# Splitting weights one unit earlier, transposing the identity while waiting, and choosing experts with a match-and-replace

## The reference

```
h = x
a = rms_norm(h, norm1);  h = h + hybrid_mixer(a)          # GLA branch + dilated window attention, gated, one output product
c = rms_norm(h, norm2);  h = h + memory_cross_attention(c, mem)   # 4 heads of 128, 256 memory tokens
f = rms_norm(h, norm3);  h = h + moe_ffn(f)               # top 4 of 32 experts, gates = softmax over the 4 logits
out = rms_norm(h, final)
```

## Time and profile before

| | |
|---|---|
| median of 3 runs | 1260.05 us (1258.52 to 1261.59) |
| the profiled execution | 1258.43 us, span of its instructions 1256.7 us |
| TensorE clock granted, mean | 0.981 |
| PE (matmul) busy | 1146.3 us, 91% |
| DVE (VectorE) busy | 412.7 us, 33% |
| ACT (ScalarE) busy | 259.6 us, 21% |
| read from HBM | 456.57 MB |

### The profile page before, as it was taken

One profiled execution on the slowest core, in us unless ns is written; L12 is line 12 of the kernel. 1 busy time (PEld: TensorE's weight loads), 2 busy tenths in 40 slices (PEclk: granted clock), 3 DMA queues, 4 the chain that ended last, 5 costly groups with the idle time before them and its releaser, 6 DMA issues.

```text
span 1256.7 us, 16017 instructions
## 1 busy us (share of the span) xinstructions
PE 1146.3 (91%) x6642; PEld 569.8 (45%) x6642; DVE 412.7 (33%) x809; ACT 259.6 (21%) x449; POOL 18.5 (1%) x41
## 2 busy tenths in 40 slices
PE   6999999998999999999889988798898999889987
PEld 5788989887433333333233322332332233223332
DVE  6689464665413221121122211211211122122113
ACT  5556464355310010010001000100110010001001
POOL 3000000000000000000000000000000000000000
PEclk9999999999999999999999999999999999999999
DMA  8464524984599999999999999999999999999995
GB/s 294 185 212 177 189 78 155 387 329 159 196 378 415 434 428 431 431 434 431 433 432 431 431 430 433 430 431 431 427 431 433 433 434 433 433 432 426 430 420 233
DMA packets 27525, 458.38 MB, mean 365 GB/s; under 512 B 3296, under 2 KB 3312, under 8 KB 7504
## 3 DMA queue, kind: packets, MB, share of 16 engines
q1 hardware_dynamic: 26496, 455.09, 86.5%
q0 software_dynamic: 832, 2.51, 0.6%
q10 hardware_dynamic: 144, 0.02, 0.0%
HBM read 456.57 MB, written 1.05 MB: 364 GB/s over the span
## 4 chain that ended last, share of the span: by engine, by line
PE 62%; DMA 25%; DVE 4%; ACT 3%; issue 2%; DVEq 0%; POOL 0%; SPq 0%; POOLq 0%; ACTq 0%
DMA ring<-in_w_gate_up 25%; PE bank L1814 24%; PE bank L1836 12%; PE bank L1413 6%; PE bank L1492 5%; PE bank L1436 5%; PE bank L1775 3%; PE bank L1765 2%; DVE ring L903 1%; PE bank L1827 1%; ACT ring L591 1%; PE bank L1552 1%; PE bank L1788 1%; PE bank L1577 0%; ACT reg_a L849 0%
## 5 line engine op out<-in xcount | busy, mean ns | idle before, releaser
L1814 PE MATMUL bank<-ring,reg_a 128*64 128x512 f32 x2032 | 461.5, 605 | 49.2 <-DMA ring<-in_w_gate_up 48.4
L1814 PEld LDWEIGHTS bank<-ring,reg_a 128*64 128x64 f32 x2032 | 145.6, 139 | 346.8 <-issue 273.0
L1836 PE MATMUL bank<-ring,reg_g 128*64 128x512 f32 x1024 | 235.2, 613 | 18.5 <-DVE reg_g L1332 17.6
L1306 DVE COPY reg_t<-bank 128x512 f32<-128x512 f32 x32 | 22.1, 692 | 600.2 <-PE bank L1814 600.2
L1836 PEld LDWEIGHTS bank<-ring,reg_g 128*64 128x64 f32 x1024 | 73.7, 141 | 158.9 <-issue 140.6
L903 DVE SCALAR_TENSOR_TENSOR ring<-ring 128x2048 f16<-128x2048 f32 x47 | 107.4, 2290 | 52.6 <-ACT ring L591 52.3
L573 ACT ACTIVATE reg_t<-bank 128x512 f32<-128x512 f32 x64 | 38.2, 597 | 415.2 <-PE bank L1814 217.8
L591 ACT ACTIVATE ring<-ring 128x2048 f16<-128x2048 f32 x47 | 89.3, 1906 | 28.5 <-PE bank L1492 20.8
L863 ACT ACTIVATE reg_g<-reg_g 128x256 f32<-128x256 f32 x64 | 26.7, 416 | 303.2 <-DVE reg_g L1323 303.1
L1775 PE MATMUL bank<-reg_t,reg_g 64*128 64x512 f32 x256 | 63.6, 615 | 5.6 <-ACT reg_t L573 5.6
L1413 PE MATMUL bank<-reg_a,ring 128*128 128x256 f16 x576 | 65.4, 275 | 0.1
(11 more groups left out here) (255 smaller groups left out, 710.0 us busy)
## 6 DMA issues: line engine op xcount, KB each, us to landing
ring<-in_w_gate_up SPq DMA_DIRECT2D x54, 4096.0 KB, 29.5
ring<-in_w_down SPq DMA_DIRECT2D x27, 4096.0 KB, 29.9
ring<-in_w_dense SPq DMA_DIRECT2D x47, 1024.0 KB, 4.9
ring<-in_w_gate_up SPq DMA_DIRECT2D x14, 2048.0 KB, 11.8
ring<-in_w_down SPq DMA_DIRECT2D x7, 2048.0 KB, 14.8
ring<-in_w_gate_up SPq DMA_DIRECT2D x12, 512.0 KB, 18.7
ring<-in_w_down SPq DMA_DIRECT2D x8, 512.0 KB, 12.5
ring<-in_w_gate_up SPq DMA_DIRECT2D x4, 1024.0 KB, 27.1
```

The source lines that it names most:

```text
L1814: ins = mm(pt[nh][col:col + 64, :], xg[:, c, j * SLOTS:(j + 1) * SLOTS], loaded(v + i, C, c), start=(c == 0), stop=(c == C - 1))
L1836: ins = mm(pt[2][64 * nh:64 * nh + 64, :], actT[:, 4 * i + c, :], w[:, nh * 512:(nh + 1) * 512], start=(i == 0 and c == 0), stop=(i == 1 a ...
```

## The change

- The units `xv1` and `xq0` change places in `HALVES`; `xt0` moves ahead of `xs2` in `FILLS` and in TensorE's program.
- TensorE transposes the identity 26 times into the last bank before the transposes of x.
- VectorE scales both tiles of x.
- VectorE's splits of units 1 to 3 come ahead of the rotary arguments, unit 4 behind them; ScalarE splits up to unit 4 ahead of the sines.
- In cross-attention ScalarE and VectorE split `xo0` one place earlier (ahead of `x_values(1)` and `x_max(0)`); `xo1` is split by ScalarE ahead of `x_queries(1)` and by VectorE between the two `out_low`. ScalarE copies head 0's transposes ahead of `x_exp(2)`.
- The mask comes from replacing the four largest logits (`match_replace`) and comparing with the logits; gates are the exponentials of all 32 logits times the mask, divided by their sum.
- Slots count from 1, so `place` isn't lowered by 1. The f16 parts of h are written in four pieces on ScalarE, the first low piece is taken ahead of the logits.

```
+WARM = 26
-HALVES += [f"mix{q}" for q in range(4)] + ["xv0", "xv1", "xq0", "xq1", "xo0", "xo1"]
+HALVES += [f"mix{q}" for q in range(4)] + ["xv0", "xq0", "xv1", "xq1", "xo0", "xo1"]
-FILLS += ["xv10", "xq0", "xv11", "xs0", "xs1", "xq1", "xs2", "xs3", "xt0", "xt1", "xpv0", "xt2", "xt3", "xpv1"]
+FILLS += ["xv10", "xq0", "xv11", "xs0", "xs1", "xq1", "xt0", "xs2", "xs3", "xt1", "xpv0", "xt2", "xt3", "xpv1"]
...
 # (ScalarE)
             act.activation(cut[0][:, 0, 0:AHEAD], raw[0][:, 0:AHEAD], ACT.Copy, scale=WS).then_inc(ahead_act, 1)
-            act.wait_ge(root_done, 1)
-            act.activation(xn[:, 1, :], h[:, 1, :], ACT.Copy, scale=st[:, 1:2]).then_inc(ahead_act, 1)
...
-            cut_ahead("q_g")
-
+            cut_ahead("v_g0")
             for i in range(2):
                 act.wait_ge(trig_in, i + 1)
                 act.activation(cs[:, i, :], trig[:, 2, :], ACT.Sin).then_inc(trig_out, 1)
...
-            cut_ahead("xv1")
+            cut_ahead("xq1", 0)
...
             x_values(0)
             x_queries(0)
+            cut_ahead("xo0", 0)
             x_values(1)
...
             x_exp(0)
             x_exp(1)
-            cut_ahead("xq1")
+            cut_ahead("xo1", 0)
             x_queries(1)
+            x_probs_T(0)
             x_exp(2)
-            x_probs_T(0)
+            x_probs_T(1)
             x_exp(3)
-            x_probs_T(1)
...
-            for t in range(TT):
-                act.activation(f16[:, 0, t], h[:, t, :].rearrange("p (c n) -> p c n", c=C), ACT.Copy,
-                               scale=st[:, 6 + t:7 + t]).then_inc(f_high, 1)
+            for part in range(2):
+                cc = slice(4 * part, 4 * part + 4)
+                for t in range(TT):
+                    act.activation(f16[:, 0, t, cc], h[:, t, :].rearrange("p (c n) -> p c n", c=C)[:, cc], ACT.Copy,
+                                   scale=st[:, 6 + t:7 + t]).then_inc(f_high, 1)
...
-                act.activation(g4[:, t, :], top[:, t, 0:TOPK], ACT.Exp, bias=st[:, 52 + t:53 + t],
-                               accum_out=st[:, 54 + t:55 + t]).then_inc(top_exp, 1)
+                act.activation(e_gate[:, t, :], logit[:, t, :], ACT.Exp, bias=st[:, 52 + t:53 + t])\
+                    .then_inc(top_exp, 1)
...
 # (VectorE)
-            dve.tensor_scalar(xn[:, 0, :], h[:, 0, :], st[:, 0:1], None, ALU.mult).then_inc(norm_xn, 1)
+            for t in range(TT):
+                dve.tensor_scalar(xn[:, t, :], h[:, t, :], st[:, t:t + 1], None, ALU.mult).then_inc(norm_xn, 1)
...
-            cut_ahead("q_g")
+            cut_ahead("k_g")
...
-            cut_ahead("k_g")
-
-            dve.wait_ge(consts, 8)
+            cut_ahead("v_g0")
+
+            dve.wait_ge(consts, 7)
...
-            cut_ahead("xv1")
+            cut_ahead("xo0", 0)
...
             x_prob(0)
             x_prob(1)
-            cut_ahead("xq1")
...
             out_low("xpv0", oxT, 0)
+            cut_ahead("xo1", 0)
             out_low("xpv1", oxT, 1)
             for n in range(2):
-                cut_ahead(f"xo{n}")
...
             routed_T(3)
+            dve.memset(ranked[:, :, 0:TOPK], -FAR)
...
             dve.wait_ge(root_done, roots[0])
+            f_low_part(0, 0)
             b = take(dve, "rl")
...
             for t in range(TT):
                 ins = dve.max(top[:, t, :], logit[:, t, :])
             link(ins)
+            dve.tensor_scalar(st[:, 52:54], top[:, :, 0], -1.0, None, ALU.mult).then_inc(top_ready, 1)
+            link(dve.memset(top[:, :, TOPK:], -FAR))
             for t in range(TT):
-                ins = dve.max_index(idx_u[:, t, :], top[:, t, :], logit[:, t, :])
+                ins = dve.match_replace(left[:, t, :], top[:, t, :], ranked[:, t, :], FAR)
             link(ins)
-            link(dve.tensor_copy(idx_f, idx_u[:, :, 0:TOPK]))
-            dve.tensor_scalar(st[:, 52:54], top[:, :, 0], -1.0, None, ALU.mult).then_inc(top_ready, 1)
-            hot, hot_g = oneh[:, 0:TT * TOPK, :], oneh[:, TT * TOPK:, :]
-            link(dve.tensor_tensor(hot, mid(iota_e[:], TT * TOPK), bc(idx_f.rearrange("p a b -> p (a b)"), E),
-                                   ALU.is_equal))
-            dve.reduce_sum(mask, hot.rearrange("p (t k) e -> p t e k", t=TT), AX).then_inc(gate_ready, 1)
-            f_lows(0)
+            dve.tensor_tensor(mask, logit, left[:, :, TOPK:], ALU.not_equal).then_inc(gate_ready, 1)
+            f_low_part(0, 1)
...
-            link(dve.tensor_scalar(place, place, -1.0, None, ALU.add))
...
+                link(dve.tensor_tensor(gate, e_gate, mask, ALU.mult))
+                link(dve.reduce_sum(st[:, 54:56], gate, AX))
                 link(dve.reciprocal(st[:, 54:56], st[:, 54:56]))
-                link(dve.tensor_tensor(g4, g4, bc(st[:, 54:56], TOPK), ALU.mult))
-                link(dve.tensor_tensor(hot_g, hot, bc(g4.rearrange("p a b -> p (a b)"), E), ALU.mult))
-                dve.reduce_sum(gate, hot_g.rearrange("p (t k) e -> p t e k", t=TT), AX).then_inc(gate_ready, 1)
+                dve.tensor_tensor(gate, gate, bc(st[:, 54:56], E), ALU.mult).then_inc(gate_ready, 1)
...
 # (TensorE)
             pe.wait_ge(consts, 1)
+            for _ in range(WARM):
+                pe.transpose(pt[BANKS - 1][:, 0:P], ident[:], ident[:])
...
             feature_major("xq1", weights("xq1"), aT, C)
+            x_transposes(0)
             x_scores(2)
             x_scores(3)
-            x_transposes(0)
             x_transposes(1)
```

More of the change, by code:

```diff
@@ L65 @@
 NEG = -1.0e30
+FAR = 3.0e38
 GLA_SCALE = DK ** -0.5
@@ L1217, in routed_T, with f_low_part @@
                                   bc(g3[:, 2 * q:2 * q + 2], T), ALU.mult).then_inc(free_bank(f"f_T{q}"), 1)
-            def f_lows(part):
+            def f_low_part(part, t):
                 cc = slice(4 * part, 4 * part + 4)
-                for t in range(TT):
-                    dve.wait_ge(f_high, t + 1)
-                    hh = h[:, t, :].rearrange("p (c n) -> p c n", c=C)
-                    dve.scalar_tensor_tensor(f16[:, 1, t, cc], hh[:, cc], st[:, 6 + t:7 + t], f16[:, 0, t, cc],
-                                             ALU.mult, ALU.subtract).then_inc(f_low, 1)
+                dve.wait_ge(f_high, TT * part + t + 1)
+                hh = h[:, t, :].rearrange("p (c n) -> p c n", c=C)
+                dve.scalar_tensor_tensor(f16[:, 1, t, cc], hh[:, cc], st[:, 6 + t:7 + t], f16[:, 0, t, cc],
+                                         ALU.mult, ALU.subtract).then_inc(f_low, 1)
             routed_T(1)
@@ L1264, in gates_and_lows @@
             def gates_and_lows():
-                f_lows(1)
+                for t in range(TT):
+                    f_low_part(1, t)
                 dve.wait_ge(top_exp, 2)
+                link(dve.tensor_tensor(gate, e_gate, mask, ALU.mult))
+                link(dve.reduce_sum(st[:, 54:56], gate, AX))
                 link(dve.reciprocal(st[:, 54:56], st[:, 54:56]))
-                link(dve.tensor_tensor(g4, g4, bc(st[:, 54:56], TOPK), ALU.mult))
-                link(dve.tensor_tensor(hot_g, hot, bc(g4.rearrange("p a b -> p (a b)"), E), ALU.mult))
-                dve.reduce_sum(gate, hot_g.rearrange("p (t k) e -> p t e k", t=TT), AX).then_inc(gate_ready, 1)
+                dve.tensor_tensor(gate, gate, bc(st[:, 54:56], E), ALU.mult).then_inc(gate_ready, 1)
             def body(n, k, z, first, last):
@@ L1463, in _ @@
             feature_major("k_g", weights("k_g"), aT, C)
-            pe.wait_ge(consts, 8)
+            pe.wait_ge(consts, 7)
             pe.wait_ge(alr_cut, 2)
@@ L1629, in _ @@
             token_major("xv0", weights("xv0"), memT, C, (0, 1), 256)
-            norm_transposes("c_T", lambda t, c: xn[:, t, c * P:(c + 1) * P], ((norm_xn, 4), (norm_xn, 5)))
+            norm_transposes("c_T", lambda t, c: xn[:, t, c * P:(c + 1) * P], ((norm_xn, 5), (norm_xn, 6)))
             w_xv1 = weights("xv1")
```

24 lines of the change are left out of this document (10 added, 14 removed).

## The result

| | before | after |
|---|---|---|
| median, on one chip | 1259.72 us (4 runs, 1258.52 to 1261.59) | 1252.14 us (4 runs, 1251.61 to 1253.44) |
| profiled execution, span | 1258.43, 1256.7 | 1252.26, 1250.5 |
| granted clock, mean | 0.981 | 0.975 |

The ratio is 0.9946, with an interval of 0.9934 to 0.9958: 5.3 to 8.3 us faster. A second measurement of the changed kernel on another chip gave 0.9945 (0.9932 to 0.9958). The forecast was 1254.5, 5.5 us less than the 1260.05 before it, in a range of 1251.5 to 1258.0.

What follows compares the result with a forecast made beforehand. The prediction took a TensorE-bound front, which releases a DMA-bound stream of expert weights, to bound the kernel. First projections -2.9, cross-attention -1.8 and routing -0.8 summed to -5.5, from 1260.05 to 1254.5 us, range 1251.5 to 1258.0.

Steps and rivals of the forecast that it cites:

- What bounds it: Whole kernel: a TensorE-bound front up to the first expert's matmuls sets when the DMA-bound weight stream at 432 GB/s starts.
- A, -2.9: First projections: reordered weight splits remove TensorE's waits at v_g1 and r_g0; -2.9 us, bounds -2.0 and -2.93.
- the tightest slack is 0.9 to 1.9 us: First projections: unit 5's low half ready at 40.0 to 41.0, needed by r_g1 at 41.89, so no new wait.
- Term: 0, whatever it gains: Start up to k_g at 20.05: normalised tiles and identity transposes gain nothing, since k_g waits for unit 1; 0 us.
- B, -1.8: Cross-attention: reordered splits and copies bring xo's late pairs sooner; -1.8 us, bounds -2.2 and -0.9.
- +0.7: Cross-attention: loss at xv10, which must wait for unit 44's low half after xq0 and xv1 change places; 0.7 us.
- C, -0.8: Routing: replacement instead of index search and one-hot makes the mask earlier; -0.8 us, bounds 0 and -1.0.
- The sum: Whole kernel: -2.9 - 1.8 - 0.8 = -5.5 us, median from 1260.05 to 1254.5.
- the likeliest case: Whole run: the forecast itself, 1254.5 us, own range 1252.6 to 1257.5 with the spread of runs; chance 0.65.
- No block failed: Rival: r_g1 waits again or x_max(0) falls on the path; 1257.4 or 1256.3 us, chance 0.2.
- The stream hid nothing: Rival: the front's gain is hidden because the expert weight stream does not start earlier; 1260 us, chance 0.07.
- The clock did not stay low: Rival: TensorE's clock stays at its lower level from q_g on, price +8 us; 1262.5 us, chance 0.03.

Runs made afterwards that it cites:

- gt_first: Changed kernel with VectorE's split of unit eg3 behind the low parts of the gated output and first two transposed-probability copies in dilated attention; 1252.41 us, ratio 0.9946.
- no_warm_slack: Changed kernel without the 26 identity transposes, unit 4 split behind the sines (ScalarE) and behind the masks (VectorE); 1251.72 us, ratio 0.9945.
- b_undone: Changed kernel with cross-attention's old order of xv1, xq0, xt0, the xo0 and xo1 splits and ScalarE's copies; 1256.13 us, ratio 0.9973.
- delay_5: Kernel of no_warm_slack with 46 more identity transposes ahead of xv0, to delay the front; 1256.74 us, ratio 0.9971.
- pad_nops: Kernel of no_warm_slack with 52 empty TensorE instructions in the place of the 26 transposes; 1254.71 us, ratio 0.9958.
- alr_late: Changed kernel with ScalarE's splits of units 1 and 2 and VectorE's of unit 1 ahead of the small weights; 1253.32 us, ratio 0.9948.
- all_three: Kernel of best with the 26 identity transposes put back; 1250.40 us, ratio 0.9934.
- best: Changed kernel without identity transposes, units 3 and 4 split behind sines and masks, q_g's high parts before small weights, gates' copy before a split; 1251.22 us, 0.9942.

## Why the prediction was right, and where it was not

- **What bounds it.** The two parts, a front that sets the start and a stream that follows at its own length, are borne out by all rows of the table: 922.5 within 1.6 by the medians, 917.6 to 920.0 in the profiled executions. The stream kept its 432 GB/s.
- **A, -2.9.** Measured -3.01 and -2.86 in the two profiles of the changed kernel and 2.96 when undone. Both waits went, none came in their place in these two (0.17 did in gt_first), and the gain passed on to 150 us.
- **A, the slack.** The step "the tightest slack is 0.9 to 1.9 us" was mis-sized: it was 0.46. I let ScalarE begin unit 4 at 25.35, when it had a free place; the load was the later, at 26.70. The table load and the sines, queued behind that split, were late by as much, and the masks came at 36.3, the late end of the 35.3 to 36.3 that I had said. From there unit 5 took 5.1 us where I had put 4.7. That the term held all the same rests on a margin of half a microsecond: it was not far from failing.
- **A, "Term: 0, whatever it gains".** `k_g` stayed at 19.98, as said. The claim holds where unit 5 has slack and `k_g` waits for the small load (no_warm_slack, 49.41). In the order of the changed kernel the one profile without the transposes was 1.05 later, not 0, since unit 4's load came later and the slack was used up; with `k_g`'s wait gone they gave 0.3. x_T's 14 transposes did get shorter in the changed kernel's first profile, 2.27 for 3.25 us, but that is not steady: of the eight profiles with the 26, five have 1.75 to 2.72 for the 14, and three have 3.78 to 3.91 for all 16, where those without have 3.50 to 3.82. The Trainium skill ("TensorE: Matmul & The Clock Gate", Part 4) has it that transposes don't count as work for the clock gate. This case speaks against it: at 0.23 each the 26 would take 6.0 us, they took 4.49 to 5.81 in the eight profiles, and TensorE had done nothing else. The shortest but one, in b_undone, with x_T behind it at the full rate:

```profile
1.59 4.52 PE L1448 MATMUL bank<-ident 128*128 128x128 f32 x26 [1.59 <-POOL ident L517]
...
9.80 1.75 PE L1443 MATMUL bank<-ident,reg_g 128*128 128x128 f32 x14 [0.23 <-DVE reg_g L945]
```
- **B, -1.8.** Measured -1.96 from `c_T` to the late pairs, with +0.61 at `xv10` in it (foretold +0.7). `x_max(0)` stood behind a split, and TensorE did not wait for it.
- **C, -0.8.** Measured -0.94 to the prefix sums, and nothing more behind them (4.68 us to the first expert product in both kernels), as said: the pieces of the f16 parts and the slots from 1 gave TensorE nothing. The replacement is 0.09 + 0.18 a pair, the 0.27 taken. The Trainium skill ("Vector Engine (DVE) Microarchitecture Reference", 3.9) tells of one steady pass, and the trace is in keeping with it: 0.18 for 36 elements, as for the search over 32.
- **The sum.** -5.5 foretold, -5.7 to -5.9 at the first expert at equal clock (330.66 and 330.82 for 336.55). The medians moved by 7.1 to 7.6, so that 1252.14 lies near the low end of the range (1251.5) and below the 1252.6 that I gave as the low end of the likeliest case. The 1.2 to 1.9 between front and medians is within the interval. In the two profiled executions of the result there is almost nothing between: they differ by 6.2, of which 5.9 is the front at equal clock and 0.3 lies behind it (918.5 and 918.2), while the fall of the clock cost each of them 1.6 to 1.7. How often the clock falls differs from execution to execution and is part of what makes single medians uncertain. Whether there is more than the front in the medians stays open.
- **The rivals.** No block failed. The stream hid nothing (delay_5, by the spans; its medians don't tell). The clock did not stay low.

## What to carry to other kernels

When a wait is removed by moving a step forward, look at what now stands behind that step on its engine, and whether the step itself waits for a load: the loads' landing, not the engine's free time, sets the slack. Where a long stream follows a front, compare kernels by the start of the stream at equal clock; it told differences of 1 us where medians of five runs on different chips can be 3 us apart with the same front (no_warm_slack and pad_nops). A stand of 7 us in the middle of a stream that is bound by DMA can cost nothing, while 1 us ahead of it costs 1 us.

## What the hardware showed that was not expected

- The granted clock fell from 2.4 to 1.2 GHz at places that change between executions of one program (173 us in one, 352 in another), each in the front or at the first `down` products, after a wait of TensorE of 1.8 to 2.4 us, at 1.2 to 1.7 us a time. Two of the 14 profiles show no such fall with the same waits, three show two. With the wait at 0.67 to 0.68 (three profiles) it did not fall at the second dilated scores; with 2.12 to 2.14 it fell there in five of eleven.
- Transposes brought the rate of TensorE up: 26 of them, with nothing before, took 4.49 to 5.81 us in eight profiles, for 6.0 at the 0.23 each of a start without them.
- TensorE stood 5.3 to 5.7 us at the exit of the first loop in the kernels without the transposes at the start, and 10.8 to 12.5 in those with them, with 40 instruction packets for 39 in every such profile and DMA at 381 to 420 GB/s from 790 to 810 us for 424 to 432. 52 empty instructions in their place, or 46 transposes elsewhere, left it at 5.65. Its cause is open; all_three against best shows that it cost nothing measurable.
- One load of 1 MB (unit 4), which left its queue at 19.95 or 20.02 us, could be used at 26.70, 27.45 or 28.15; in alr_late it left at 18.00 and could be used at 28.13.
